# In each attention step VectorE combines the two differential probabilities ahead of the maximum of the MLA scores

## What is computed

```
def _sdpa(q, k, v, scale):                       # MLA
    s = jnp.einsum('bqhd,bkhd->bhqk', q, k).astype(F32) * scale
    p = jax.nn.softmax(s, axis=-1).astype(v.dtype)
    return jnp.einsum('bhqk,bkhd->bqhd', p, v)

def _diff_sdpa(q1, q2, k1, k2, v, scale, lam):   # differential
    p1 = jax.nn.softmax(jnp.einsum('bqhd,bkhd->bhqk', q1, k1).astype(F32) * scale, axis=-1)
    p2 = jax.nn.softmax(jnp.einsum('bqhd,bkhd->bhqk', q2, k2).astype(F32) * scale, axis=-1)
    return jnp.einsum('bhqk,bkhd->bqhd', (p1 - lam * p2).astype(v.dtype), v)
```

## Time and profile before

| | |
|---|---|
| median of 3 runs | 2922.47 us (2920.8 to 2928.03) |
| the profiled execution | 2926.13 us |
| its span in the trace | 2924.4 us |
| TensorE busy | 2843.9 us, 97% |
| VectorE busy | 1668.9 us, 57% |
| ScalarE busy | 884.9 us, 30% |
| L1681, the 120 maxima | 100.4 us, 842 ns each |
| L1230, the 120 exponentials | 97.9 us, 817 ns each |

### The profile page before, as it was taken

One profiled execution on the slowest core, in us unless ns is written; L12 is line 12 of the kernel. 1 busy time (PEld: TensorE's weight loads), 2 busy tenths in 40 slices (PEclk: granted clock), 3 DMA queues, 4 the chain that ended last, 5 costly groups with the idle time before them and its releaser, 6 DMA issues.

```text
span 2924.4 us, 43919 instructions
## 1 busy us (share of the span) xinstructions
PE 2843.9 (97%) x16990; PEld 2434.4 (83%) x16990; DVE 1668.9 (57%) x3117; ACT 884.9 (30%) x1370; POOL 106.6 (4%) x82
## 2 busy tenths in 40 slices
PE   6999999999989999999999999999999999999998
PEld 4888888888756788888888888888888756898996
DVE  5876687733467578757876335443443477443443
ACT  4221122233256442212223221122233256422232
POOL 0000000034000000000000000000024000000000
PEclk8999999999999999999999999999999999999999
DMA  6444334322300134433342213221222300233332
GB/s 226 125 126 123 107 119 137 110 56 65 82 1 1 33 111 122 127 117 115 122 124 84 65 57 117 70 65 57 70 68 71 82 1 1 87 93 96 90 98 68
DMA packets 422760, 255.40 MB, mean 87 GB/s; under 512 B 26017, under 2 KB 418057, under 8 KB 422666
## 3 DMA queue, kind: packets, MB, share of 16 engines
q1 hardware_dynamic: 422160, 254.00, 29.2%
q10 hardware_dynamic: 506, 0.13, 0.0%
HBM read 252.01 MB, written 2.10 MB: 87 GB/s over the span
## 4 chain that ended last, share of the span: by engine, by line
PE 94%; DVE 3%; ACT 2%; issue 1%; DMA 0%; SPq 0%; DVEq 0%; ACTq 0%
PE pair L686 56%; PE pair L680 26%; PE pair L949 2%; PE pair L903 2%; PE pair L917 1%; PE pair L926 1%; PE pair L650 1%; PE pair L881 1%; PE pair L934 1%; PE pair L863 1%; DVE lo_w L1371 0%; PE pair L869 0%; PE pair L874 0%; ACT hi_w L1029 0%; DMA x_tok<-in_ctx 0%
## 5 line engine op out<-in xcount | busy, mean ns | idle before, releaser
L686 PE MATMUL pair<-n_hi,hi_w 128*128 128x260 f32 (+2 forms) x3456 | 847.9, 326 | 18.0 <-DVE n_lo L1410 11.9
L686 PE MATMUL pair<-n_hi,lo_w 128*128 128x258 f32 (+2 forms) x3456 | 845.5, 325 | 0.0
L686 PE MATMUL pair<-n_lo,hi_w 128*128 128x256 f32 (+1 forms) x3456 | 845.1, 325 | 0.0
L686 PEld LDWEIGHTS pair<-n_hi,hi_w 128*128 128x128 f32 x3456 | 532.7, 189 | 81.6 <-issue 11.0
L686 PEld LDWEIGHTS pair<-n_hi,lo_w 128*128 128x128 f32 x3456 | 537.1, 190 | 58.3
L686 PEld LDWEIGHTS pair<-n_lo,hi_w 128*128 128x128 f32 x3456 | 535.0, 189 | 55.1
L1371 DVE TENSOR_TENSOR lo_w<-raw_w,hi_w 128x1024 fp32r<-128x1024 f32 (+1 forms) x296 | 394.4, 1333 | 302.2 <-ACT hi_w L1029 301.5
L1029 ACT CAST hi_w<-raw_w 128x1024 fp32r<-128x1024 f32 (+1 forms) x296 | 328.9, 1111 | 653.4 <-PE pair L686 365.3
L1543 DVE SCALAR_TENSOR_TENSOR mod_acc<-mod_w,silu_c,mod_acc 128x256 f32<-128x256 f32 x896 | 364.6, 478 | 0.0
L1466 DVE TENSOR_TENSOR buf<-pair,rstd 128x512 f32<-128x512 f32 (+1 forms) x308 | 164.9, 571 | 309.0 <-PE pair L686 309.0
L680 PE MATMUL pair<-h_hi,hi_w 128*128 128x512 f32 x1232 | 338.7, 345 | 0.0
(11 more groups left out here) (186 smaller groups left out, 1958.9 us busy)
## 6 DMA issues: line engine op xcount, KB each, us to landing
raw_w<-in_ffn_w SPq DMA_DIRECT2D x176, 512.0 KB, 3.8
mod_w<-in_w_mod SPq DMA_DIRECT2D x64, 1024.0 KB, 5.1
raw_w<-in_ffn_w SPq DMA_DIRECT2D x64, 704.0 KB, 4.6
raw_w<-in_w_in SPq DMA_DIRECT2D x38, 512.0 KB, 3.9
raw_w<-in_w_out SPq DMA_DIRECT2D x16, 512.0 KB, 4.2
pro_scale<-in_w_mod SPq DMA_DIRECT2D x2, 2048.0 KB, 15.3
pro_shift<-in_w_mod SPq DMA_DIRECT2D x2, 2048.0 KB, 13.3
x_tok<-in_x SPq DMA_DIRECT2D x4, 512.0 KB, 5.4
```

Of the source, the lines that this page charges most:

```text
L686: mm = pe.matmul(pair[s][:, a:a + m], wt[:, k * P:(k + 1) * P], src[:, of(k):of(k) + m], start=opens, stop=closes)
```

## The change

In VectorE's loop the call of `combine_diff(c)` is placed ahead of `maxima(c, 2)`. Both functions, their waits and their signals stay as they are, and so do the other queues.

```diff
                     if c - 3 in pieces:
                         low_mla(c - 3)
                     if c < n_steps:
+                        combine_diff(c)
                         maxima(c, 2)
-                        combine_diff(c)
                         if c % 2 and c >= 3:
                             scale_mla(c - 2)
```

## The result

The changed kernel takes 2954.52 us (median of 4 runs, 2953.32 to 2958.5), the kernel before 2923.71 us (4 runs, 2920.8 to 2928.03). The ratio is 1.0107, 95% interval 1.0089 to 1.0124: 30.8 us slower, where 28.6 were forecast. The span of the profiled execution grew by 32.3 us, from 2924.4 to 2956.7.

The account below looks back on a forecast made before the run. The prediction took TensorE to bound the attention loops. Its terms, 15.4 + 2.5 + 5.8 + 2.6 + 2.3, sum to 28.6 us, giving 2951 us from the 2922.47 median, range 2935 to 2962.

Parts of the forecast that it names:

- No gain from an earlier combination: VectorE, large steps: the combination starts when exponential 1 is done, before and after, so gain 0; bounds 0 to 8.7 us.
- Even step: Large even step, t counted from its first maximum: exponential 2 late, TensorE's next MLA scores 0.8 us late.
- Odd step: Large odd step: turn_inverse, scale_mla and second half of next scores wait behind exponential 2; 1.4 us a pair, 15.4 over 11.
- First pairs: First pair of steps in each layer: only VectorE's own late end counts, 1.25 us each, 2.5 in all.
- Second pairs: Second pair of each layer: 1.4 us plus 1.5 for probabilities_mla behind a late exponential 2; 2.9 each, 5.8 in all.
- First large pair behind the small steps: Layer 0, first large pair after the small steps, 11.58 us before: the VectorE-ScalarE chain makes it 2.6 us longer.
- Small steps: Layer 0, keys 256 wide, two groups of four: 0.15 us for a group's first pair, 1.0 for its second; 2.3 in all.
- hidden delay: Rival: TensorE's real slack hides exponential 2's delay; at most 0.5 us a pair, 8 us, 2922 to 2931; chance 0.07.
- The even term alone: Rival: turn_inverse and scale_mla keep close to their place, only the MLA scores' 0.8 us counts; 13 us, 2935; chance 0.09.
- second channel: ScalarE's queue in odd steps: turn_inverse and probabilities_mla stand behind late exponential 2, scale_mla and the scores' second half behind these.
- The faster rival: Rival: in small steps and those with low_mla the earlier combination gains up to 8.7 us, 2914; chance 0.03.
- The clock: Rival: TensorE's short pauses in each pair lower its granted clock; 4.4 us a pair, 70 us, about 3021; chance 0.03.

## Why the prediction was right, and its terms

The forecast was 2951 us in a range of 2935 to 2962; 2954.5 came. The mechanism was right, and the runs above show it; that the sum came so close is in part luck. By its steps:

- *No gain from an earlier combination*: right. It starts at t=3.82 (3.81 before); the small steps alone gave none either.
- *Even step*: 6.13 us, forecast 6.1; MLA scores at t=7.35, forecast 7.3. The pause is 0.69 us, forecast about 0.8. Shown by the pause of 0.69 us and by the run with even steps alone.
- *Odd step*: exponential 2 at t=12.42 (forecast 12.39), turn_inverse at 13.31 (13.37), scale_mla at 13.60 (13.67), the weights at 13.94 (14.01). The pair came to 14.68, not 14.85, so the term was **1.24, not 1.4**. Two small things: turn_inverse starts 0.89 us after the exponential ahead of it (2435.19, 2436.08), 0.10 before its sum is all read out, where I took 0.98; and the next first maximum stands 0.74 us behind the weights instead of 0.84, since TensorE is no longer at work on the first half when they load. Over 11 pairs that is 13.6 instead of 15.4. The pause in the matmuls is 0.31 us, forecast about 0.6, and TensorE is busy 93%, forecast 90%.
- *First pairs*: 835.38 to 847.75 in layer 0 is 12.37 us, 1.86 more than 10.51; 1.33 more in layer 1 (12.20). Forecast 1.25 each. The nearness shows nothing, since the clock was at half for longer in these pairs than in the trace of before, and it was so in runs with the order of before too: with one unused column the first pair of layer 0 takes 11.90 us, and with the change in the small steps alone that of layer 1 takes 11.89. Against these the change adds 0.47 and 0.31. The changed order with the extra maximum in lam_sum, at half clock for under 2 us, takes 11.58 and 11.57: 1.07 and 0.70 more than before. So the order's own part is 0.3 to 1.1 us a pair, below the term.
- *Second pairs*: 16.69 us in layer 0, 3.11 more than 13.58; 3.40 in layer 1; forecast 2.9, and its extra part was shown by the run that turned ScalarE's queue round.
- *First large pair behind the small steps* (911.67 to 925.82): 14.15 us, 2.57 more; forecast 2.6.
- *Small steps*: the first group of four takes 18.74 us, 1.31 more; forecast 1.15.

From first to last first-maximum layer 0 grew by 17.5 us and layer 1 by 11.2, 28.6 together. The other 3.7 of the span are, rounded, 2.0 ahead of the first loop, 1.0 less between the loops and 2.8 behind the last maximum, which holds the last step's own delay.

That the loops grew by just the forecast sum is luck. The forecast counts the last pair of layer 1, which lies behind the last maximum, and its steady pairs were too long by 0.16 us each. What made up for it is the clock: 1.6 us in the second group of small steps and, by the comparison above, 1.4 to 2.4 us in the two first pairs. Without these stretches the loops would have grown by about 25 us, an estimate from the same traces.

The rivals: the hidden delay didn't happen. The rule of the Trainium skill that the prediction weighed (page "Perfetto Trace Analysis", section "Identifying the Most-Contended Engine": the share of LDWEIGHTS rather than matmul busy time) would have made it likely, with 71% in the earlier trace rows; but 1.24 us a pair came through, and the share is 65% now. The even term alone is what a pair costs without the second channel, as the run with ScalarE's queue turned round shows: 14.04 us a pair, 0.60 more than before. The faster rival fell with the small steps, and its bound of 8.7 us was a misreading: matmuls had waited 1.2 us for the combination.

*The clock* was right for the steady pairs and missed elsewhere. Over the large steps of layer 1 it stays at 1.00, pauses of 0.7 us and all. But the first row below, in the second group of small steps, is at half; the same steps were at 1.00 in the kernel before, and a pause of 1.55 us stands ahead of it (second row). The third row is the first pair of layer 0 in the changed kernel, and the fourth the same pair in the run with one unused column, which has the order of before:

```profile
972.00:975.00 3.00, 3.00 (x15) 3.00 (x16) 1.45 (x6) 0.82 (x3) 0.00 (x0) 0.50 0.00 0
...
969.94 0.85 PE L926 MATMUL pair<-ident,buf 128*128 128x128 f32 x6 [1.55 <-ACT proj L1248]
...
839.00:842.00 3.00, 3.00 (x13) 1.83 (x10) 2.75 (x3) 0.99 (x2) 0.00 (x0) 0.50 0.00 0
...
848.50:851.50 3.00, 3.00 (x13) 1.79 (x10) 1.93 (x2) 0.24 (x2) 0.00 (x0) 0.50 0.00 0
```

The step around the first row took 7.06 us, where the same step of the first group, at full clock, took 5.43: 1.6 us. The step ahead of it took 8.03 instead of 7.68, but was over before the clock fell, and these 0.35 us are unexplained. The stretch at half stands at this place in all four traces in which the large odd steps have the changed order and ScalarE's queue the old one, behind pauses of 1.20 to 1.98 us, and in none of the other ten; the run with probabilities_mla first has one in the first group instead (from 889.5 us). Yet pauses of 1.20 and 1.62 us at the same place of the first group, and one of 2.50 us in layer 0's second pair of the changed kernel (at 849.75), left the clock at 1.00. So the change seems to bring the stretch on, but a pause of that length alone does not; no run tried it by itself. The rule of the Trainium skill named in the prediction (page "TensorE: Matmul & The Clock Gate", section "A second HAM failure mode: psum-queue depth-cycling": frequent short idling lets the clock swing) would fit that stretch. It doesn't fit the steady pairs, which have two short pauses each, 0.69 and 0.31 us, and stay at 1.00.

## What to carry to other kernels

Before an instruction is moved ahead of another on an in-order engine, ask what the engine would be waiting for at that moment: work that fills the wait is free where it is, and becomes late by the wait and the moved work together. The wait alone, moved with no work behind it, cost something else here: it made the combination late. Then follow the delayed result into the queue that takes it, and see what stands behind it there; here turn_inverse and probabilities_mla, which have nothing to do with the moved work, stood behind exponential 2, and 18 of the 31 us went when they were put ahead of it. A walk of three queues with the durations of one trace, and checked first against the old order, gave the loss within a tenth, but in the profiled execution some 3 to 4 us of it were the clock's: a sum that comes out right has to be compared term by term.

## What was not expected of the hardware

One unused column of 4 bytes costs the kernel before 32.7 us, 16 columns 19.1. The steady pairs don't move (13.44 us in both), and TensorE is busy throughout; the sweeps got slower. All runs have the same 16990 matmuls. From the last step of layer 0 to the first of layer 1, first maximum to first maximum, the kernel before takes 1395.6 us, with one column 1417.9, with 16 columns 1408.4. Not every sweep loses: behind the last step of layer 1 the run with one column is 5.6 us faster than before. Busy time from 1500 to 2000 us, in the kernel before, then with one column, then with 16:

```profile
1500.00:2000.00 500.00, 500.00 (x2880) 437.47 (x2879) 239.92 (x433) 116.34 (x147) 0.00 (x0) 1.00 0.27 79
```

```profile
1500.00:2000.00 500.00, 500.00 (x2832) 432.63 (x2831) 247.24 (x453) 115.25 (x145) 0.00 (x0) 1.00 0.27 80
```

```profile
1500.00:2000.00 500.00, 500.00 (x2848) 434.09 (x2848) 243.53 (x444) 114.86 (x145) 0.00 (x0) 1.00 0.27 79
```

TensorE finishes 2880, 2832 and 2848 matmuls in the same 500 us at the same granted clock (the windows are equal in time and so hold not quite the same work). A matmul of the sweep at L686 lasts 332 to 334 ns in the mean from 1400 to 2200 us, and 338 to 340 with one column. The place of the tiles in the memory is all that differs, and alignment to 4 or 64 bytes alone doesn't explain it, since the shift by 64 bytes costs too. Which tiles or addresses meet is open. An experiment on such a kernel must not add a tile ahead of the others, or needs a run with the tile alone.
